# Three tile groups instead of two in a fused Mamba/attention/PEER layer

## The reference, cut to what matters

```python
x = x + token_mixer(rmsnorm(x))       # xn @ w_in (1024 x 3080), two causal convolutions, SSD scan, @ w_out
x = x + cross_attn(rmsnorm(x), k, v)  # w_mq, softmax over 256 memory tokens, w_mo; k, v = rmsnorm(mem) @ w_mk, w_mv
x = x + peer(rmsnorm(x))              # w_pq (1024 x 2048), scores against sub_keys, 8 heads, top 16 of 128 x 128 experts
y = rmsnorm(x)
# peer, per token t, head h: hid = gelu(x[t] . u_tab[e]), out[t] += softmax(score) * hid * v_tab[e] over its 16 experts e
```

## Time and profile before

| | us |
|---|---|
| median of 3 runs (lowest, highest) | 1919.24 (1911.52, 1919.64) |
| the profiled execution | 1920.86 |
| its span, first to last instruction | 1918.8 |
| TensorE busy, clock granted on average | 1707.1, 0.943 |
| VectorE, ScalarE, GpSimd busy | 1245.2, 371.5, 734.2 |
| moved by the queues | 563.10 MB |

### The profile page before, as it was taken

The page is one execution under the profiler, slowest core; times in us unless marked ns, Lnnn a source line. Parts: engine busy times, 40 slices in busy tenths (PEclk is TensorE's granted clock), DMA queues, the critical chain, the costliest instruction groups (busy, mean ns, idle before and its releaser), DMA issues. The chain is left out here.

```text
span 1918.8 us, 19965 instructions
## 1 busy us (share of the span) xinstructions
PE 1707.1 (89%) x7088; PEld 1263.9 (66%) x7088; DVE 1245.2 (65%) x2560; ACT 371.5 (19%) x914; POOL 734.2 (38%) x597
## 2 busy tenths in 40 slices
PE   6998999989659998988686999999999999999854
PEld 5887788868546776877574666666666666666321
DVE  1252211798679767998996999676555555555773
ACT  2032023102421235523452001101000000000001
POOL 0000000223024437513774555455554555545650
PEclk9999999999769998999888999999999999999977
DMA  5533433768138959967999999999999999999992
GB/s 161 182 117 110 154 110 110 262 219 308 33 121 294 342 163 341 339 221 287 336 415 377 380 394 400 398 356 399 401 399 399 389 400 398 397 390 393 405 350 88
DMA packets 238301, 563.10 MB, mean 293 GB/s; under 512 B 17068, under 2 KB 125276, under 8 KB 236156
## 3 DMA queue, kind: packets, MB, share of 16 engines
q0 software_dynamic: 82944, 302.03, 41.6%
q1 hardware_dynamic: 152956, 243.04, 35.7%
q10 hardware_dynamic: 2304, 16.78, 2.1%
HBM read 539.46 MB, written 21.66 MB: 292 GB/s over the span
## 5 line engine op out<-in xcount | busy, mean ns | idle before, releaser
L750 POOL DMA_INDIRECT M<-in_u_tab,IDX x288 | 366.6, 1273 | 797.1 <-DVE PEER L1675 408.3
L1064 PE MATMUL PSB<-M,HST 128*128 128x512 f32 x1024 | 466.2, 601 | 51.6 <-DVE HST L1754 49.7
L757 POOL DMA_INDIRECT M<-in_v_tab,IDX x288 | 364.0, 1264 | 340.7 <-DVE X L1696 252.0
L1056 PE MATMUL PSB<-XN,M 128*128 128x256 f32 x2048 | 467.6, 382 | 6.9 <-DMA M<-in_u_blocks 5.9
L1056 PEld LDWEIGHTS PSB<-XN,M 128*128 128x128 f32 x2048 | 391.4, 192 | 105.9 <-issue 56.6
L1064 PEld LDWEIGHTS PSB<-M,HST 128*128 128x128 f32 x1024 | 196.5, 193 | 259.5 <-issue 247.0
L1675 DVE CUSTOM_DVE_ANT_0 M<-M,XN 128x1024 f32<-128x1024 f32 x288 | 350.4, 1220 | 17.8 <-DMA M<-in_u_tab,IDX 17.2
L799 PE MATMUL PSB<-M 128*128 128x256 f32 (+1 forms) x1408 | 337.8, 402 | 11.9 <-DVE M L1345 10.6
L1696 DVE SCALAR_TENSOR_TENSOR X<-M,PEER,X 128x1024 f32<-128x1024 f32 x256 | 328.0, 1281 | 5.8 <-DMA M<-in_v_tab,IDX 3.3
L799 PEld LDWEIGHTS PSB<-M 128*128 128x128 f32 x1408 | 273.3, 196 | 70.0 <-DVE M L1345 11.5
L806 PE MATMUL PSB<-M 128*128 128x256 f32 (+1 forms) x1056 | 241.9, 389 | 0.0
(11 more groups left out here) (208 smaller groups left out, 1030.9 us busy)
## 6 DMA issues: line engine op xcount, KB each, us to landing
M<-in_u_blocks SPq DMA_DIRECT2D x128, 512.0 KB
M<-in_v_tab SPq DMA_DIRECT2D x128, 512.0 KB
M<-in_w_in SPq DMA_DIRECT2D x24, 1024.0 KB
M<-in_w_pq SPq DMA_DIRECT2D x16, 1024.0 KB
gate_spill<-M ACTq DMA_DIRECT2D x16, 1024.0 KB
M<-gate_spill SPq DMA_DIRECT2D x16, 1024.0 KB
M<-in_w_out SPq DMA_DIRECT2D x8, 1024.0 KB
M<-in_w_mq SPq DMA_DIRECT2D x8, 1024.0 KB
```

The source lines that it names most:

```text
L750: pool.indirect_dma_start(out=UA[:, s % RR, :], out_offset=None, in_=utab, in_offset=bass.IndirectOffsetOnAxis(ap=IDX[:, n:n + 1], axis=0) ...
L757: pool.indirect_dma_start(out=VA[:, s % RR, :], out_offset=None, in_=vtab, in_offset=bass.IndirectOffsetOnAxis(ap=IDX[:, n:n + 1], axis=0) ...
L1056: last = pe.matmul(PSB[:, 4 + b % 2, 0:2 * P], UBLK[:, b % SR, c, :], XN[:, 1:3, c * P:(c + 1) * P], start=(c == 0), stop=(c == DC - 1))
L1064: last = pe.matmul(PSB[:, 2 * t + hf, :], WR[:, b % WRING, t * P:(t + 1) * P], VBLK[:, b % SR, hf * 512:(hf + 1) * 512], start=(b == 0), s ...
```

## The change

The groups become tile 0; tiles 1 and 2; tile 3 with the sample. All group-dependent sizes, waits, history copies and loads are generalised from two groups to three, so every weight block is streamed three times. Group 1 reloads the prompt's K and V from the outputs. Of the 16 memory products, in group 0: three go between the last convolutions, five into the one scan chain, two before the attention transposes, six between attention scores and values. Weight blocks are ordered by first use. Both DENSE tiles are in group 1; their routers and batches become fillers of group 2. The planner's costs of in, q and pq depend on the group. Tile 2's scores move to the one-hot buffer, and "tt" is an ordinary job for both tiles.

```diff
-TG = [[0, 1], [2, 3, 4]]
+TG = [[0], [1, 2], [3, 4]]
-NG = [2 * P, 2 * P + SAM]
+WG = [P, 2 * P, P]
+NG = [P, 2 * P, P + SAM]
...
+    kv = [("kv", kv, q, mt) for kv in range(2) for q in range(4) for mt in range(2)] * (g == 0)
     for c in range(3, 8):
-        n = int(g == 0 or c < 5)
-        s += z[:n] + [("cs", g, c)]
-        z = z[n:]
+        s += z[:int(c < 5)] + [("cs", g, c)] + kv[c - 5:c - 4] * (c >= 5)
+        z = z[int(c < 5):]
+    s += soft_chain(TG[g], [[], kv[3:5], kv[5:7], kv[7:8]] if g == 0 else [[], z[0:1], z[1:2], [], [], [], [], []])
...
-    s += [("norm", 1, t) for t in TG[g]]
+    s += [("norm", 1, t) for t in TG[g]] + kv[8:10]
...
-        s += [("a1", t)] + ([("a2", TG[g][i - 1])] if i else [])
+        s += [("a1", t)] + kv[10:16] + ([("a2", TG[g][i - 1])] if i else [])
...
-EARLY_STEPS = 5
-G0_STEPS = 2
+SLOT_SHARE = 3
+LK_EVERY, AFTER, BEFORE_W = 6, 5, 12
+def pe_us(x):
+    if x[0] in ("in", "q", "pq"):
+        return (2.2, 3.9, 2.7)[x[1]]
+    return PE_US.get(x[0], 0.0)
...
-    out, work = work[:lead], work[lead:] + dense(1)
+    out, work = work[:lead], [work[lead:] + dense(1), dense(2)]
...
+    extra = first[:4] + merged(first[4:], slots[:one]) + slots[one:]
+    hot = [x for t in DENSE for h in range(PH) for x in rt(t, h)]
+    hot = [hot[:4 * PH] + soft(1) + hot[4 * PH:] + soft(2), batches(1) + batches(2)]
...
+    for part in range(2):
+        if part == 1:
+            n_slots = (len(hot[0]) + len(hot[1]) // 2) // SLOT_SHARE
+            n_first = n_slots * len(hot[0]) // (len(hot[0]) + len(hot[1]) // 2)
+            later = extra[n_slots:]
+            extra = merged(hot[0], extra[:n_first]) + [("tt", 1), ("tt", 2)] + merged(hot[1], extra[n_first:n_slots])
+        for w in work[part]:
...
+    for n, x in enumerate(extra):
+        while k < min(HRING - AFTER, n // LK_EVERY):
+            out.append(ahead[k])
+            k += 1
+        out.append(x)
+    out += ahead[k:]
+    slots = later
+    out += slots[:BEFORE_W]
+    slots = slots[BEFORE_W:]
...
+BLOCKS = [(w, c, uses[-1][1]) for (w, c, _), uses in sorted(USES.items(), key=lambda x: x[1][0][0])]
...
+                if i == BLOCK_AT[("w_pq", BW, 0)]:
                     wait_drained(sp, ("kv", 1, 3, 1))
                     sp.dma_start(o["mv"].rearrange("l b (t p) h d -> p (l b t) (h d)", p=P), V0).then_inc(outs, 16)
                 if i == BLOCK_AT[("w_mq", 2 * BW, 1)]:
+                    wait_job(sp, ("o", 1, 3, TG[1][-1]))
+                    sp.wait_ge(outs, 16 * 2)
+                    sp.dma_start(KB[0], o["mk"].rearrange("l b (t p) h d -> p (l b t) (h d)", p=P)).then_inc(kb_in, 16)
+                if i == BLOCK_AT[("w_mo", BW, 1)]:
+                    wait_job(sp, ("kt", 1, 0, 3))
+                    sp.dma_start(VV[:, 0], o["mv"].rearrange("l b (t p) h d -> p (l b t) (h d)", p=P)).then_inc(vv_in, 16)
...
             if t == 2:
-                return SCB[:, b, :]
+                return OHF[:, 512 * b:512 * (b + 1)]
```

More of the change, by code:

```diff
@@ L55, in group @@
 def group(t):
-    return int(t in TG[1])
+    return [t in tiles for tiles in TG].index(True)
 def pos(t):
@@ L86, in dense @@
     else:
-        s += [("turn", 0, t) for t in TG[1]]
+        s += [("turn", 0, t) for t in TG[g]]
     for b in ("gc", "v", "gb", "x0"):
@@ L119, in dense @@
     s += [("norm", 2, t) for t in TG[g]] + [("sk", g, q) for q in range(4)] + [("turn", 2, t) for t in TG[g]]
[L120 to L123, removed]
+    s += [("keep_x", t) for t in TG[g] if t in DENSE]
+    if g < LAST:
+        s += [("norm", 0, t) for t in TG[g + 1]]
     for m in range(16):
@@ L126, in dense @@
         if m % 4 == 0 and m:
[L127 to L130, removed]
+            s += [("sc", t, m // 4 - 1) for t in TG[g]]
+    s += [("sc", t, 3) for t in TG[g]]
     return s
@@ L194, in plan @@
     slots += [("add", GSTEPS - 1)]
-    step = lambda i: slots.index(("d", i, 0))
-    one, early, mid, last = step(1), step(3), step(EARLY_STEPS), step(EARLY_STEPS + G0_STEPS)
     first = [x for h in range(PH) for x in rt(0, h)] + soft(0)
-    second = [x for h in range(PH) for x in rt(1, h)] + soft(1)
-    extra = first[:4] + merged(first[4:], slots[:one]) + merged(second, slots[one:early])
-    extra += [("tt", 1)] + merged(batches(1), slots[early:mid])
-    late_slots, slots = slots[mid:last], slots[last:]
+    one = slots.index(("d", 1, 0))
@@ new lines, in plan @@
+    gone, held = set(out), []
+    for part in range(2):
[5 more added lines that the diff above has]
+        for w in work[part]:
+            if w[0] in LONG:
+                out += held
+                t_pe += sum(PE_US["gb"] for x in held if x[0] == "gb")
+                held = []
+            while extra and w[0] in LONG and t_dve < t_pe:
+                x = extra[0]
+                if x[0] == "rt" and ("sc", x[1], x[2] // 2) not in gone:
+                    break
+                if x[0] in ("oh", "tt") and held:
+                    break
+                extra.pop(0)
+                if x[0] in ("gb", "tt"):
+                    held.append(x)
+                    continue
+                out.append(x)
+                t_dve += dve_us(x)
+            out.append(w)
+            gone.add(w)
+            t_pe += pe_us(w)
+            t_dve = max(t_dve, t_pe - 10) + dve_us(w)
@@ L237, in plan @@
     out += held
     ahead = [("lk", b) for b in range(HRING)]
-    out += merged(merged(late, extra), ahead[:4]) + merged(rt(2, 6) + rt(2, 7), ahead[4:8]) + ahead[8:9] + soft(2)
-    out += ahead[9:10] + late_slots[:3] + [("tt", 2)]
-    g0, n = [], P // OH_TOK
-    for k in range(0, n, 2):
-        g0 += [("oh", 2, k), ("oh", 2, k + 1)] + ahead[10 + k * 13 // n:10 + (k + 2) * 13 // n] + [("gb", 2, k), ("gb", 2, k + 1)]
-    g0 += ahead[23:]
-    out += merged(g0, late_slots[3:])
+    n = len(extra) // (HRING - AFTER)
@@ L1021, in tt @@
                 parts = [I12[:, t - 1, 0, :], I12[:, t - 1, 1, :], GATE[:, t, :, :].rearrange("p h k -> p (h k)")]
-                if t == 1:
-                    transposes(("tt", 1), parts)
-                    return
-                settle()
-                pe.wait_ge(g_out, nbank[0])
-                for k in range(3):
-                    last = pe.transpose(PSB[:, 7, k * P:(k + 1) * P], parts[k], ident[:, :])
-                last.then_inc(tt_done, 1)
+                transposes(("tt", t), parts)
             def gb(t, n):
```

199 lines of the change are left out of this document (76 added, 123 removed).

## The result

The changed kernel takes 2011.12 us (median of 4 runs, 2006.99 to 2013.2), the kernel before in the same comparison 1917.3: a ratio of 1.0491, 95% interval 1.0461 to 1.0522. The forecast was 1938 us with a range from 1893 to 1970. The side was right, the size was not: the median lies 41 us above the range. The profiled execution took 2011.91 us, span 2010.2, against 1918.8.

What follows compares the result with a forecast made beforehand. TensorE was taken to bound the expert-block loop, with the dense layers setting when it begins. Loop start 1060, loop 857 and end 19 gave a 1936 span, 1938 us (+1.0%), range 1893 to 1970.

Steps and rivals of the forecast that it cites:

- First group: Group 0 cut to one tile: narrow jobs take half the time, 120 us saved, first score job near 218 us.
- rival 2: Narrow jobs cost more than half, by weight loads or late blocks: 35 us more, 1973; chance 0.08.
- Weight traffic: Third pass over the weights, 32 more blocks of 1 MB: priced at nothing in group 0.
- Where the fillers land: Planner's placement of router pieces, slots and batches before the block loop: 202 slots, 6 fewer than before.
- Group 1 until its scan ends: From 218 us, VectorE's work of 125 us at 94%: scan starts at 350, output projections at 391.
- Group 1 from there: Output projections to group 2: TensorE 200, queues 213, GpSimd 209; taken as 214 us, group 2 starting at 605.
- Group 2: Third group's dense part, summed stage by stage as engines alternate: 305 us, ending at 910.
- Look-ahead stretch: 46 gate batches and 24 first products before the loop: 150 us against 186, loop starting at 1060.
- Loop and tail: Expert-block loop with 374 slots instead of 368, adding 3 us: loop 857, end 19.
- Rival 1: Early start pays, queues and VectorE absorb group 1: loop starts 45 us earlier, 1893; chance 0.26.
- Rival 3: Block loop becomes bound by its transfers: 8 to 15 us more, 1952; chance 0.07.
- Rival 4: Filler placement differs from the walk, or gains and losses cancel: 1920; chance 0.07.

Runs made afterwards that it cites:

- e5: Changed kernel (three groups) with no dots or weighted adds before the last score job, all moved to the loop: 2159.28 us.
- e12: Changed kernel with the row fetches of steps 0 to 4 bringing half the bytes, their number unchanged: 1998.64 us.
- e4: Changed kernel with a slot (dot or weighted add) priced 1.75 us until group 2, moving 37 slots out of the part before it: 2046.34 us, ratio 1.0657.
- e1: Changed kernel with SP's spill wait and three gate-group reads moved seven look-ahead products down: 2004.49 us, ratio 1.0464.
- e2: Changed kernel with each look-ahead product between a pair's two one-hots and two gate batches, in 17 pairs: 1989.5 us, ratio 1.0366.
- e3: Changed kernel with all 24 look-ahead products placed after the last gate batch: 2050.3 us.
- e11: Changed kernel with look-ahead products inside the batch pairs and gate reads later on SP's queue, no slot moved: 1970.18 us, ratio 1.0287.
- e7: Changed kernel with later gate reads, products inside batch pairs, and 46 slots and two router heads moved from loop into look-ahead stretch: 1974.07 us, ratio 1.0291.
- e6: Kernel before (two groups) with no dots or weighted adds before the last score job, all moved to the loop: 2071.86 us.

## Why the prediction missed

**First group, 218 us.** Right (213.8). Twelve narrow jobs take 21.60 us, 1.80 each against the 1.79 forecast, so the halving of the earlier trace rows holds and rival 2 falls. By the spacing that the Trainium skill gives for 128 columns ("TensorE: Matmul & The Clock Gate", Back-to-back issue gap) the 44 jobs would have cost some 35 us more, an estimate; the row at 38.25 is against it, as those of before were.

**Weight traffic at nothing.** Right as far as shown: in group 0 TensorE waits 2.1 us for a weight block, its three waits for w_pq blocks in group 1's second part are 5.8 us together, and e5's queues are half idle.

**Where the fillers land.** Right: the plan has 109 dots and 93 adds before the loop, the 202 of the walk.

**Group 1 until its scan ends.** 391 against 387.4.

**Group 1 from there: 214, measured 242.** The bytes were right (86.5 forecast, 87.40 MB moved), the rate was right where the queues are full, and the bound was wrong in kind: the forecast took the longest of three resources, TensorE's 200, the queues' 213 and GpSimd's 209. None of them is busy throughout: TensorE 191, GpSimd 169 of 242 us, and the queues fall under 320 GB/s in seven bins of 40. Without any slot (e5) the part takes 188 us, from 378.1 to 566.0, so the slots cost some 54. e12 shows 16 to 21 of them to be bytes; some 16 stand in ScalarE's order behind one gelu, a wait of TensorE that is gone in e4 and e5 together with the slots, but that no run took away by itself. The remaining 17 to 22 stay open; VectorE's share of them (119 slots among its dense work) was not tried by itself. The forecast put scaled drains behind VectorE's waits and did not look at ScalarE's queue. The stated bound of 240 us is 2 short.

**Group 2: 305.** Measured 300; it is the term that was worked stage by stage, and it held.

**Look-ahead stretch: 150, measured 211. This is the step that failed**, 61 of the 74 us by which the span exceeds the 1936 of the sum. The forecast put two things next to each other and didn't queue them. It said that the wait for the first gate group "goes under those seven products"; it does, but SP waits for the same spill, with 3 MB of reads, ahead of the u blocks of those products: 21 us of the 61 (e1). And it took "5.8" for a cycle of two batches and a product, "between TensorE's 3.45 + 2 x 0.89 = 5.2 and 7.0", arguing that fewer slots relieve GpSimd. e2 shows 5.24 to be reachable with the product between one-hots and batches; the diff's every sixth filler puts it in a place where it lengthens the closed loop of one-hot, scaling, batch and copy: 35 us (e2). A pair without a product was taken at 4.5 us; that is near the 4.74 that e3 shows at the full clock, but e3's other pairs take 5.7 and 6.2 at 0.60, and the forecast did not price the clock. With both repaired the stretch is 158.6 (e11): the resources' sum was sound, the order was not read.

**Loop and tail.** 857 + 19, measured 870 together. Six more slots cost nothing that shows here; 38 more cost 70 us (e4), by waits for u blocks, and 46 fewer save nothing to 5 us (e7 beside the changed kernel and beside e11).

**Rival 1** (loop start 45 us earlier) has a slip in its sum: a loop start at 1001 with the same 857 and 19 gives 1879, and the 1893 took the 45 off 1938 instead of off the kernel before. It fell at group 1, which it wanted free at 200; e5, without any slot, is the only kernel near it (188 us). **Rival 3** did not happen at 374 slots and did at 412. **Rival 4**: placement was as walked.

Why the change loses at all: the early start it buys (group 1 at 248 instead of 392) is spent on the same work at worse terms. The third group itself costs 47 us (e5, e6), the look-ahead stretch 22; the 24 between them are put down to denser fillers, as what is left of 71.6, and rest on runs on different chips.

## What to carry to other kernels

A stretch bounded by "the slowest engine's busy time" is a lower bound only; before trusting it, write out each in-order queue (ScalarE and the DMA-issuing engine too) in the new order and ask what stands behind every wait that the change moves. A job that fits the gap of a small closed loop across three engines costs a fraction of its length there (0.5 of 3.46 us at the full clock) and more elsewhere, so its place decides, not its length alone. And before giving a loop more or less filler, try both ways: here 46 slots taken out saved little or nothing and 38 put in cost 70 us.

## What was not expected of the hardware

The gate batches alone ran at a mean granted clock of 0.65 (940 to 1065 in e3, TensorE busy 74.5 of 125 us) and took 3.75 us for sixteen matmuls; with products among them (e2, busy 110.5) the clock was 0.89 and they took 1.95. A product in the gap thus also pays for itself by keeping TensorE at the higher of its two levels: e2's pairs without a product, 1032 to 1065, run at 0.59.

The 128-column float32 products are spaced 21.60/192 = 0.1125 us, half of the 256-column ones, each with a weight load of its own: no sign that the load sets the pace.
